# Recurrent heads: tanh written to the product's bank, head gate on GpSimd, forward values and query cast on ScalarE, the next query's projection between the score tiles

## The reference, cut to what matters

```
qk = silu(centred_short_conv(concat([ml_q, ml_k]), conv_w, conv_b))   # 5 taps
h_fwd = mlstm(mq, mk, mv, i_f, f_f)
h_bwd = flip(mlstm(flip(mq), flip(mk), flip(mv), flip(i_b), flip(f_b)))
# each way: num / max(|den|, exp(-m)), a weighted sum over earlier (later) tokens
hm = (h_fwd + h_bwd) * sigmoid(ml_o)
mu = mean(hm); var = mean((hm - mu)**2)          # per token and head
ml_out = (hm - mu) * rsqrt(var + EPS) * ml_norm_w * silu(ml_z)
y = concat([na_out, ml_out]) @ w_out
```

## Time and profile before

| | us |
|---|---|
| median of 3 runs | 1194.45 (1192.84 to 1195.0) |
| the profiled execution: its own time | 1193.18 |
| its span in the profile | 1191.4 |
| recurrent heads and output projection in the span | about 1008 to 1168 |

### The profile page before, as it was taken

How to read it: one execution, slowest core, us unless ns; L and a number is a source line. 1 busy time by engine, 2 the same in 40 slices (tenths; PEclk the granted TensorE clock), 3 DMA queues, 4 the chain that set the end, 5 groups by cost and what they waited for, 6 DMA issues and landing times.

```text
span 1191.4 us, 19865 instructions
## 1 busy us (share of the span) xinstructions
PE 1109.2 (93%) x7408; PEld 905.0 (76%) x7408; DVE 766.0 (64%) x1608; ACT 643.5 (54%) x1339; POOL 349.8 (29%) x194
## 2 busy tenths in 40 slices
PE   3899999999998799999999999999999989998896
PEld 0587778877886589887687878798777778886785
DVE  6466666676658526364877877636877775638855
ACT  4614455555556426642766768746567653435723
POOL 1532112211120224663300003215432224434651
PEclk9899999999999999999999999999999999998999
DMA  9641334322112221231222021133221405312102
GB/s 360 239 155 58 144 132 147 144 103 101 40 28 89 73 71 37 71 119 59 56 90 63 28 81 46 49 113 102 67 60 47 155 10 153 88 61 90 53 19 71
DMA packets 34251, 109.32 MB, mean 92 GB/s; under 512 B 4516, under 2 KB 7076, under 8 KB 33772
## 3 DMA queue, kind: packets, MB, share of 16 engines
q1 hardware_dynamic: 34156, 108.05, 27.2%
HBM read 101.39 MB, written 2.11 MB: 87 GB/s over the span
## 4 chain that ended last, share of the span: by engine, by line
PE 67%; DVE 18%; ACT 7%; issue 4%; DMA 2%; POOL 1%; SPq 0%; DVEq 0%; POOLq 0%; ACTq 0%
PE PS L669 26%; PE PS L652 13%; PE PS L785 7%; PE PS L773 6%; PE PS L963 5%; PE PS L1024 2%; PE PS L704 2%; DMA AF<-wstream 2%; PE PS L869 1%; ACT AF L1238 1%; DVE AF L1910 1%; DVE AD L2285 1%; DVE AF L1989 1%; DVE PS L2262 1%; DVE AR L2186 1%
## 5 line engine op out<-in xcount | busy, mean ns | idle before, releaser
L669 PE MATMUL PS<-AR 128*128 128x512 f32 (+1 forms) x2208 | 454.4, 363 | 12.0 <-DVE AR L1969 4.7
L2454 POOL TENSOR_TENSOR AR<-AF,AR 128x1024 fp32r<-128x1024 f32 x99 | 242.3, 2453 | 662.4 <-ACT AR L1115 662.4
L669 PEld LDWEIGHTS PS<-AR 128*128 128x128 f32 x2208 | 367.0, 191 | 80.2 <-issue 16.2
L652 PE MATMUL PS<-AR 128*128 128x256 f32 (+4 forms) x1284 | 247.0, 329 | 15.9 <-DVEq L2336 5.3
L652 PEld LDWEIGHTS PS<-AR 128*128 128x128 f32 (+1 forms) x1284 | 181.7, 191 | 52.8 <-issue 21.4
L1247 ACT ACTIVATE AF<-PS 128x512 f32<-128x512 f32 (+3 forms) x192 | 124.4, 649 | 105.7 <-PE PS L773 101.6
L1238 ACT ACTIVATE AF<-PS,AF 128x512 f32<-128x512 f32 (+3 forms) x192 | 140.7, 733 | 29.9 <-DVE AF L2262 20.9
L773 PE MATMUL PS<-AF 128*128 128x128 f32 x864 | 128.0, 275 | 10.8 <-DVE AF L1910 7.2
L1115 ACT ACTIVATE AR<-AF 128x1024 fp32r<-128x1024 f32 x99 | 103.4, 1052 | 45.9 <-PE PS L963 30.1
L773 PEld LDWEIGHTS PS<-AF 128*128 128x128 f32 x864 | 100.2, 141 | 35.7 <-issue 14.9
L785 PE MATMUL PS<-AF 128*64 128x128 f32 x1728 | 116.0, 279 | 5.1 <-DVE AF L1917 5.1
(11 more groups left out here) (202 smaller groups left out, 1169.7 us busy)
## 6 DMA issues: line engine op xcount, KB each, us to landing
AF<-wstream SPq DMA_DIRECT2D x171, 512.0 KB, 4.5
AF<-x_in SPq DMA_DIRECT2D x2, 1024.0 KB, 8.4
AD<-rows SPq DMA_DIRECT2D x4, 512.0 KB, 5.7
out<-AF SPq DMA_DIRECT2D x16, 128.0 KB, 1.9
AF<-AF SPq DMA_DIRECT2D x28, 64.0 KB, 2.0
AF<-rpb_band SPq DMA_DIRECT2D x8, 224.0 KB, 4.9
BIAS<-rpb_band SPq DMA_DIRECT2D x8, 224.0 KB, 4.5
AF<-ctx_in SPq DMA_DIRECT2D x1, 1024.0 KB, 5.2
```

The source lines that it names most:

```text
L652: mm = pe.matmul(out, stationary, moving, start=i == 0, stop=i == len(products) - 1)
L669: mm = pe.matmul(out[:, 0:t1 - t0], a, b, start=k == 0 and i == 0, stop=k == nk - 1 and i == 2)
L2454: pool.tensor_tensor(w[:, 1, :], raw(c), w[:, 0, :].bitcast(F32), ALU.subtract).then_inc(lo_done, 1)
```

## The change

- The tanh of the convolved product goes to the PSUM bank of the projection (whose last reader had been the convolution) instead of to the buffer `TQ`. The bank counts as read after `doubled_silu`.
- The rounding of the query moves from VectorE to ScalarE (`query_high`). The key's stays.
- The forward values are scaled by ScalarE in four instructions of 128x128 (`forward_values`); VectorE only makes the denominators and adds the backward values. There are two denominator buffers.
- The head gate of heads 0 to 2 is a product on GpSimd (`gate_head`); the `+ 1` of the gate is put in once for all by four more ScalarE instructions in `all_gates`. The last head's gate stays on VectorE.
- `centre(h-1)` and `turned_head(h-2)` move into `weigh(h, 0)`, after its second tile. The z gate moves behind the convolution of q.
- On ScalarE `conv_tanh` of q moves behind `conv_input` and the chunk cast of k. Squares and roots of head h-1 move into the middle of the backward decays, and `output_gates` in front of the forward decays. The cast that `need("D.z3", 4)` asks for moves from before to behind the backward decays of the last head; the four `out_high` move to in front of its forward decays.
- On TensorE the next query's projection (in the last head `output(0, 0, 2)`) stands between score tiles 1 and 2.
- On GpSimd two `output_low` and the head gate stand in the loop over the heads.

```diff
 TensorE
+                score_head(0)
+                score_head(1)
+                if not last:
+                    project(f"D.q{h + 1}.x", f"D.q{h + 1}", HC, 0, S)
+                else:
+                    output(0, 0, 2)
                 if h >= 2:
                     turn_head(h - 2)
+                score_head(2)
+                score_head(3)
                 if not last:
-                    project(f"D.q{h + 1}.x", f"D.q{h + 1}", HC, 0, S)
                     project(f"D.k{h + 1}.x", f"D.k{h + 1}", HC, 0, S)
                 else:
-                    output(0, 0, 4)
+                    output(0, 2, 4)
...
 ScalarE
-                act.activation(TQ, CV[:, i], ACT.Tanh, scale=0.5).then_inc(tq_ready, 1)
+                act.activation(bank[tasks[f"D.{what}{h}.x"][0]], CV[:, i], ACT.Tanh, scale=0.5).then_inc(tq_ready, 1)
+            def query_high(h):
+                b, i = tasks[f"D.q{h}.x"]
+                act.wait_ge(acc_read[b], i)
+                act.activation(QM[:, h % 2, 0], CV[:, 0], ACT.Copy).then_inc(qm_hi, 1)
...
+            def backward_decay(h):
+                decay(h, 1, 0, 2)
+                if h >= 1:
+                    centred_squares(h - 1)
+                    head_root(h - 1)
+                decay(h, 1, 2, QT)
...
             for h in range(N_ML - 1):
-                decay(h, 1)
+                backward_decay(h)
                 conv_input(h + 1, "q")
                 need(f"D.q{h + 1}", 4)
-                conv_tanh(h + 1, "q")
                 conv_input(h + 1, "k")
                 need(f"D.k{h + 1}", 4)
-                if h >= 1:
-                    centred_squares(h - 1)
+                conv_tanh(h + 1, "q")
+                query_high(h + 1)
                 conv_tanh(h + 1, "k")
-                if h >= 1:
-                    head_root(h - 1)
+                forward_values(h)
+                output_gates(h + 1)
+                if h + 1 == N_ML - 1:
+                    for j in range(4):
+                        out_high("C", j, OB, [(OG, 0, S)])
                 decay(h + 1, 0)
-                output_gates(h + 1)
...
-            for j in range(4):
-                out_high("C", j, OB, [(OG, 0, S)])
-            need(f"D.z{N_ML - 1}", 4)
             act.wait_ge(ml_done, 1)
             out_high("C", 4, OB, [(OG, 0, S)])
-            decay(N_ML - 1, 1)
-            centred_squares(N_ML - 2)
-            head_root(N_ML - 2)
+            backward_decay(N_ML - 1)
+            need(f"D.z{N_ML - 1}", 4)
+            forward_values(N_ML - 1)
...
 VectorE
+                weigh(h, 0, 0, 2)
+                if h >= 1:
+                    centre(h - 1)
+                if h >= 2:
+                    turned_head(h - 2)
+                weigh(h, 0, 2, QT)
+                weigh(h, 1)
             for h in range(N_ML - 1):
                 scored_head(h)
-                if h == 1:
-                    gate_head(0)
-                    centre(0)
                 convolve(h + 1, "q")
+                gate_z(h)
                 doubled_silu(h + 1, "q")
                 convolve(h + 1, "k")
+                denominators(h, 0)
                 doubled_silu(h + 1, "k")
                 if h >= 1:
                     finish(h - 1)
-                divide(h, 0)
-                divide(h, 1)
+                denominators(h, 1)
+                add_backward(h)
...
 GpSimd, end of the loop over h = 1 to 3 (after low_m(h, "k"))
-                if h < N_ML - 1:
-                    need(f"D.z{h}", 4)
+                if h == N_ML - 1:
+                    output_low(0)
+                    output_low(1)
                 if h == 1:
+                    need("D.z1", 4)
                     need("D.k2", 1)
+                gate_head(h - 1)
+                if h == 2:
+                    need("D.z2", 4)
...
-            for j in range(4):
+            for j in range(2, 4):
                 output_low(j)
             need(f"D.z{N_ML - 1}", 4)
             for j in range(4, KD - 2):
```

More of the change, by code:

```diff
@@ L433, in build @@
         CV = tiles(R3F, 2, S)
-        TQ, XD = R3F[:, 2056:2568], tiles(R3F[:, 2568:], 2, QT, P)
+        XD = tiles(R3F[:, 2568:], 2, QT, P)
         W = tiles(AD[:, 7936:], 4, S)
@@ L444, in build @@
         DV = PPW[:, 6:8]
-        HEAD_SQ, HEAD_R, DENOM, HEAD_SUM, HEAD_T = (STAT[:, i] for i in range(5))
+        HEAD_SQ, HEAD_R, HEAD_SUM, HEAD_T = (STAT[:, i] for i in (0, 1, 3, 4))
+        DENOM = [STAT[:, 2], OGC_[:, 1984:1988]]
         HALF_B = OGC_[:, 1856:1872]
@@ L1581, in _ @@
             need("D.z0", 1)
+            query_high(0)
             conv_tanh(0, "k")
@@ L1593, in all_gates @@
                     act.wait_ge(o_biased, i + 1)
-                    act.activation(TOK[:, t], TOK[:, t], ACT.Tanh, scale=0.5).then_inc(o_gate, 1)
+                    act.activation(TOK[:, t], TOK[:, t], ACT.Tanh, scale=0.5).then_inc(tok_tanh, 1)
+                for i in range(QT):
+                    t = GATE_ORDER[i]
+                    act.wait_ge(tok_tanh, i + 1)
+                    act.activation(TOK[:, t], TOK[:, t], ACT.Copy, bias=1.0).then_inc(o_gate, 1)
             def output_gates(h):
@@ L1615, in head_root, with forward_values @@
                 one_over_root(HEAD_R, HEAD_SQ, P, 4 * EPS)
+            def forward_values(h):
+                act.wait_ge(den_ready, h + 1)
+                if h >= 1:
+                    act.wait_ge(dv_ready, h)
+                for t in range(QT):
+                    ins = act.activation(HM[:, t * P:t * P + P], weighed(0)[:, t // 2, t % 2, 0:P], ACT.Copy,
+                                         scale=DENOM[0][:, t:t + 1])
+                    if t % 2:
+                        read(ins, f"D.n{h}.f{t // 2}")
+            def backward_decay(h):
[4 more added lines that the diff above has]
+                decay(h, 1, 2, QT)
             output_gates(0)
@@ L2286, in convolve @@
                                                    ALU.mult, ALU.add)
-                    step(ins) if tap < 4 else read(ins, name)
+                    step(ins)
                 ends = CV[:, i].rearrange("p (a b) -> p a b", b=2)[:, ::S // 2 - 1, :]
@@ L2295, in doubled_silu, with weigh @@
                 dve.wait_ge(tq_ready, 2 * h + i + 1)
[L2296 to L2302, removed]
+                name = f"D.{what}{h}.x"
+                read(dve.scalar_tensor_tensor(CV[:, i], bank[tasks[name][0]], 1.0, CV[:, i], ALU.add, ALU.mult), name)
+                if what == "k":
+                    dve.tensor_copy(KM[:, h % 2, 0], CV[:, i]).then_inc(km_hi, 1)
+            def weigh(h, way, i0=0, i1=QT):
+                if h >= 1 and i0 == 0:
                     b, i = tasks[f"D.n{h - 1}.{('f1', 'b0')[way]}"]
                     dve.wait_ge(acc_ready[b], i)
-                for i, j in enumerate(key_tiles(way)):
+                for i, j in list(enumerate(key_tiles(way)))[i0:i1]:
                     acc = wait_acc(f"D.s{h}.{j}")
@@ L2313, in weigh, with denominators @@
                         dve.sem_inc(acc_read[j], 1)
[L2315 to L2319, removed]
+            def denominators(h, way):
+                for b in range(2):
+                    wait_acc(f"D.n{h}.{'fb'[way]}{b}")
                 acc = weighed(way)
                 den, floor = acc[:, :, :, P], EMCOL[:, way, :, h].rearrange("p (b i) -> p b i", b=2)
-                d = DENOM.rearrange("p (b i) -> p b i", b=2)
+                d = DENOM[way].rearrange("p (b i) -> p b i", b=2)
                 if h == 0 and way == 0:
@@ L2538, in low_m @@
                 i = "qk".index(what)
-                pool.wait_ge(qk_hi, 2 * h + i + 1)
+                pool.wait_ge((qm_hi, km_hi)[i], h + 1)
                 dst = (QM, KM)[i][:, h % 2]
```

77 lines of the change are left out of this document (41 added, 36 removed).

## The result

The changed kernel takes 1201.49 us (median of 7 runs, 1198.33 to 1204.53) against 1194.45 (7 runs, 1192.84 to 1195.01): ratio 1.006, 95% interval 1.0042 to 1.0077. It is 7 us slower. The forecast was 1201.

What follows compares the result with a forecast made beforehand. TensorE, busy 93% of the span, bounds the kernel, so the result is the last turn's shift: 3.6 us late at full clock plus 3.9 of clock loss, +7.5 on 1193.18, said 1201. Range 1196 to 1204 (62%), 8 in 10 1194 to 1207.

Steps and rivals of the forecast that it cites:

- the walk: Head-by-head pricing of the change on all engines from 1008 us on; sum +7.5 us at the last turn.
- each station: Starts along TensorE's timeline: head 1 1.1 late, head 2 2.9, head 3 1.1, backward product 4.8 at full clock.
- the backward product: TensorE's backward `weigh_head` in the last head: starts at 1134.0, 4.8 us late.
- the last turn: TensorE's turn at 1146.17, on which all later work hangs: 3.6 late at full clock, +7.5 with clock loss.
- the last head: Head 3's start to its backward product: 17.5 us instead of 13.8, so +3.7.
- The last step: Profiled 1193.18 + 7.5 gives 1200.7; the median of the runs lies 1.3 above the profiled execution; said 1201.
- z1, z2, z3: TensorE's z projections of heads 1 to 3 wait for VectorE's product, which frees q's bank: about 1, 4.7, 2.4 us.
- the chain given for z2: Copies, GpSimd gate, centring, squares to root, exponentials, taps and casts, table load, tanh, product; ends at 1081 against 1076.3 wanted.
- The cast of C.o2: Moved behind the last head's backward decays on ScalarE; output slice 4 waits over 3 us for GpSimd.
- two pauses: TensorE's waits of over 4 us at z2 and the output slice cost the clock 1.7 + 2.2 = 3.9 us.
- a rival: Longer: z3's wait costs the clock too (+1.9), VectorE meets GpSimd (+2 to 4); 1204 to 1209, 15%.
- Tail: Backward product to last turn: TensorE's own work 15.8 us where it took 17.0, so −1.2.
- That is the gain: Query's projection before tiles 2 and 3 covers waits of 2.34 and 2.92 us, with the slow clock behind them.

Runs made afterwards that it cites:

- the run with centre and root late: Changed kernel with centre(h-1) back behind both weigh calls and squares and root behind the tanh of k; 1197.80 us, ratio 1.0030.
- q's tanh early: Changed kernel with ScalarE's tanh of q again right behind its chunk cast, before the middle tap and cast of k; 1202.78 us, ratio 1.0066.
- all four orders of before: Changed kernel with TensorE's tiles together, q's tanh before k's tap, centre and root behind the scores, and the cast of C.o2 early; 1194.95 us, ratio 1.0004.
- the run with the early cast: Changed kernel with the cast of C.o2 on ScalarE again in front of the last head's backward decays; 1197.25 us, ratio 1.0024.
- without the cover: Changed kernel with TensorE's order of before: four score tiles, then the query's and the key's projection; 1204.21 us, ratio 1.0080.
- The run on the kernel before: Kernel before with only TensorE's new order: query's projection, in the last head two output slices, between tiles 1 and 2; 1205.87 us, ratio 1.0096.
- the version with both parts: Kernel before with the key's tanh in its projection's bank and VectorE's divisions of head h in front of finish(h-1); 1190.69 us, ratio 0.9969.

## Why the prediction was right

- *Size and side.* 1201 forecast, 1201.49 measured. The route was right too: the table above follows the walk within 1.6 us at each station. The stations up to the backward product were underpriced by 0.4 to 1.6, the last turn was overpriced by 1.1.
- *Luck.* That the number fits within 0.5 us is in part luck. Up to head 3 the walk is 1.6 short; the last head then took 2.6 longer than before for a forecast of 3.7, and from the backward product to the last turn TensorE was 0.6 quicker where −1.2 and 2.2 of clock were forecast. So misses of +1.6 and −2.7 cancel in part, and the shift in the stretch was 6.4 for a forecast of 7.5. The last step, from 1200.7 to 1201, takes 0.3 of the 1.3 by which the median lay above the profiled execution.
- *z1, z2, z3.* Forecast waits 1.1, 4.7, 2.4; measured 0.94, 4.94, 2.36. The middle of the chain given for z2 (wait for the gate, centring, squares, root) is shown by the run with centre and root late, which takes away 2.3 of it. Its end is not: I led it over ScalarE's casts and load, which were ready 0.94 before VectorE's convolution and its blocked edge fix, and with q's tanh early the wait stays at 4.92. That both ways were nearly as long is why the 4.7 fits. For z3 the order of q's tanh is the cause, as said: 1.6 of 2.4 go with it. For z1 only 0.4 of the 0.9 go; the rest comes with tiles 2 and 3 reaching VectorE later, for with q's tanh early and the tiles together z1 doesn't wait (all four orders of before).
- *Last head.* The cast of C.o2 was named as what slice 4 waits for: shown, 4.64 became 0.40.
- *Slow clock.* I priced two pauses, at z2 and slice 4. Three came: z3 took 7.18 for 5.6 behind only 2.36 of waiting, 1.6 us that I had in a rival. Head 3's station shows it (4.4 for 2.8). It belongs to this execution: behind the same wait z3 took 5.75 in the run with the early cast. At slice 4 the clock cost 0.7 + 0.7 (1.62 for 0.94, 3.06 for 2.39) instead of 2.2.
- *Tail.* Forecast −1.2, measured 16.3 against 17.0: −0.7, and the slow `weigh_head` is in it (0.7).
- *The step that failed.* I wrote of TensorE's new order "That is the gain". Alone it is an 11 us loss. The walk has no term for tiles 2 and 3 reaching VectorE later, and its sum was right all the same: in the changed kernel other things are late anyway, and without the cover z1, z2 and z3 wait exactly as long, while the waits before tile 2 come back (median 2.7 higher). The run on the kernel before says what the cover does when nothing else is late.
- *Port.* The product with one input in PSUM took 0.69 in all eight cases, as said (I gave 0.75). That the rounding behind it would meet GpSimd (0.43 to 2.33) I had not seen. It cost nothing here: TensorE, at its low clock, reached head 2 later than the key's low part. The difference in `centre`, which I had always blocked behind the gate, took 0.69 in head 1, where GpSimd stood idle behind the gate, and 0.98 in the last head.

What stays open: how much each of the four orders costs by itself, since they don't add up (4.2, 3.7, −1.3 and −2.7 one by one, 6.5 together), and why the clock falls behind a wait in one execution and not in the next.

## What to carry to other kernels

A projection put in front of other tiles to cover a bank's wait delays whoever reads these tiles; look at what that reader does next, before counting the wait as won. Here the same waits went by reading the banks earlier (two calls swapped on VectorE), which moves no producer. And a cast or copy at the end of an engine's list is not idle filler: name its reader and what stands before it after the move.

## What the runs showed of the hardware

- After an idle time of 1.98 to 2.36 us on TensorE the granted clock fell in some places (12 tiles in 4.68 instead of 2.7; z3 in 7.18) and not in others: z3 took 5.75 behind the same 2.36 in the run with the early cast. The early cast's kernel is the same up to there. Behind 2.93 z3 took 5.75 too (centre and root late). In the version with both parts 9 matmuls took 4.01 behind a wait of only 0.76, with 1.46 and 1.23 shortly before; the granted clock was 0.57 there. The length of a wait alone doesn't tell it.
- The time of VectorE's rounding (one input in SBUF, 128x512) rose from 0.43 to 2.33 us beside a GpSimd subtraction of 128x1024; a reduction over SBUF stayed at 0.69 beside GpSimd's instructions. A product with one input in PSUM stayed at 0.69 as well, and an edge fix of 128x4 with both inputs in SBUF rose from 0.17 to 2.28.
- A table load on ScalarE took 1.28 us, and the tanh behind it started 0.02 after its end (1111.63 and 1112.93). It is started ahead of the wait of the instruction that needs it: at 1077.69 for a tanh that began at 1081.51.
